# Reading the high and low slots of h by turns from two halves of the tile

## The chip, the cores and the metric

The kernel runs on one core of a Trainium2 chip. The metric is the device time of one execution in microseconds (us); before the change three runs took 3407.76, 3419.19 and 3421.75 us, the median is 3419.19. An execution taken by the hardware profiler stands beside them. Engines are named as the profile names them: PE is TensorE's matmul, PEld its weight load, DVE is VectorE, ACT is ScalarE, POOL is GpSimd, SP is SyncE, which issues the DMAs.

## The reference, cut to what matters

A model of two layers on 256 tokens and 1024 features, followed by two more blocks with large feed-forward parts. Each of the first two layers ends in a product-key expert stage. That one holds the change:

```python
def peer_ffn(x, norm_ffn, w_query, sub_keys, expert_down, expert_up):
    xn = rmsnorm(x, norm_ffn)
    ...
    q = (xi @ w_query).reshape(B, PEER_CHUNK, PEER_HEADS, 2, PEER_HALF)
    s = jnp.einsum('bthpd,hpnd->bthpn', q, sub_keys)
    s1, i1 = lax.top_k(s[..., 0, :], PEER_TOPK)
    s2, i2 = lax.top_k(s[..., 1, :], PEER_TOPK)
    ...
    g = jax.nn.softmax(top_s.astype(jnp.float32), axis=-1)
    u = jnp.take(expert_down, idx, axis=0)
    act = jax.nn.gelu(jnp.einsum('btd,bthkd->bthk', xi, u).astype(jnp.float32))
    v_sel = jnp.take(expert_up, idx, axis=0)
    return jnp.einsum('bthk,bthkd->btd', (g * act).astype(xi.dtype), v_sel)
```

There are 16384 experts, of which each token picks 16 in each of 8 heads. The kernel gathers nothing: it works through all experts densely, and the softmax weights of those not picked are zero.

## The kernel before, in words

The function `peer` runs once per layer. Its last stage is `peer_experts`, and it has two halves. In the down stretch the 16384 rows of `expert_down` are taken in 128 tiles of 128 experts; each gives a 128 x 256 tile of scores (experts by tokens), which goes through the GELU and is multiplied by the routing weights. The results stand in the tile `h`, 128 tiles of 256 tokens in fp32. In the up stretch `h` is multiplied by `expert_up`: 128 tiles again, each adding to all of the output `o_ps`, eight chunks of 128 features by 256 tokens, which fill four of the accumulator memory's eight banks, two chunks in each.

Products are made in fp32r, a one-pass form of fp32 that keeps fewer bits. To keep the accuracy each operand is cut in two, a high part (`cut_hi` on ScalarE, line 234, a copy that rounds) and a low part (`cut_lo`, line 238, the difference), and three products are added: high by high, high weights by low, low weights by high.

One tile n of the up stretch goes like this. SyncE loads 512 KB of `expert_up` into one of four slots `raw` (line 1163) once VectorE has made the low part that last read the slot. ScalarE first cuts h's tile (`cut_h`, into one of two slots `h_hi`), then the weights (into one of two slots `hi`). It waits for `out_sum`, that is for TensorE to have finished tile n - 2, whose slots it writes over. GpSimd makes `h_lo`, VectorE makes `lo` of the weights. TensorE's `accumulate` waits for the high weights and the low slot of h, makes 16 matmuls (lines 1244 and 1246: for each of eight chunks of features the high weights stand in the array, and first h_hi and then h_lo streams through), waits for the low weights and makes 8 more (line 1249). Each of the 24 matmuls has its own weight load of 128 columns and streams 256 columns of tokens.

Beside that, VectorE computes the modulation vectors of a later block from 72 more loads of 512 KB (line 1456), two products a load for the first 40 loads in layer one, one product otherwise. The first four tiles of `raw` are loaded ahead.

Where things lie: `h_hi` and `h_lo` have no tile of their own but use the normed input `K.xp`, whose content the up stretch needs no more. It is made of 2 x 8 chunks of 256 fp32r values per partition; `h_hi` is chunks 0 and 1 of the first half, `h_lo` chunks 0 and 1 of the second. A slot is 1024 consecutive bytes. The constants `LINE = 512` and `MOVED = 192` see to it that the tiles of a stage (`hi` and `lo` among them) start on multiples of 512 bytes, counted alike, and `K.xp` 192 bytes past one. A weight load reads 512 bytes per partition, from a multiple of 512.

Of the kernel before, what the change touches and what calls it, by code (L numbers as in the profile page):

```python
# [16 lines left out]
P = 128  # L17
D = 1024
DC = D // P
T = 256  # L20
# [68 lines left out]
def moving_tile(nc, stack, name, shape, dt=F32R):  # L89

    stack.enter_context(nc.sbuf_tensor(f"{name}_before", [P, MOVED // 4], F32))
    tile = padded(nc, stack, name, shape, dt, LINE)[0]
    stack.enter_context(nc.sbuf_tensor(f"{name}_after", [P, (LINE - MOVED) // 4], F32))
    return tile


class Stage:
# [135 lines left out]
def cut_hi(act, hi, v):  # L233
    return act.activation(hi, v, ACT.Copy)  # L234


def cut_lo(eng, lo, v, hi):
    return eng.tensor_tensor(lo, v, hi.bitcast(F32), ALU.subtract)  # L238
# [810 lines left out]
def peer_experts(nc, K, name, layer, dram, raw, ring):  # L1049
# [23 lines left out]
    with stage(nc, f"{name}_e") as st:  # L1073
# [9 lines left out]
        hi_up, lo_up, hi_h, lo_h, out_sum = (st.sem(x) for x in ("hi_up", "lo_up", "hi_h", "lo_h", "out_sum"))  # L1083
        hi = st.sb("hi", [P, 2, D], F32R)
        lo = st.sb("lo", [P, 2, D], F32R)
        h = st.sb("h", [P, NK, T])
# [12 lines left out]
        s = key_scores(ring)  # L1099
# [9 lines left out]
        top = choice[:, 2].rearrange("p (t h j) -> p t h j", t=TT, h=PH)  # L1109
        hots = [ring[:, i].rearrange("p (n a e) -> p n a e", n=2, a=TOKS) for i in range(RING)]  # L1110

        h_hi, h_lo = K.xp[:, 0, 0:2], K.xp[:, 1, 0:2]
        s_ps = st.ps("s", [P, D])
        c_ps = st.ps("c", [P, D])
        o_ps = st.ps("o", [P, DC, T])
# [68 lines left out]
        @block.tensor  # L1184
        def _(pe):

            def score(n, k, lo_sem, before, freed=None, freed_before=0):
                if freed is not None:
                    pe.wait_ge(freed, n - (RAWS - 1 + freed_before))
                pe.wait_ge(hi_down, n + 1)  # L1190
                out = s_banks[k]
                for c in range(DC):
                    w = hi[:, k % 2, c * P:(c + 1) * P]
                    pe.matmul(out, w, K.xp[:, 0, c], start=c == 0, stop=False)  # L1194
                    pe.matmul(out, w, K.xp[:, 1, c], start=False, stop=False)  # L1195
                pe.wait_ge(lo_sem, n + (1 - before))
                for c in range(DC):
                    mm = pe.matmul(out, lo[:, k % 2, c * P:(c + 1) * P], K.xp[:, 0, c], start=False, stop=c == DC - 1)  # L1198
                mm.then_inc(product, 1)

            for k in range(RAWS):
                score(k, k, lo_pool, 0)
            with pe.Fori(1, NS // RAWS) as i:
                for k in range(RAWS):
                    score(i * RAWS + k, k, lo_pool, 0, gelued)
            for n in range(NS, TURN_AT):
                score(n, n % RAWS, lo_vector, NS, gelued)
            pe.wait_ge(chosen, 1)
            for n in range(2):
                for t in range(TT):  # L1210
                    pe.transpose(t_ps[:, n, t * P:(t + 1) * P], pick[:, n, t], K.ident[:])
            for t in range(TT):
                mm = pe.transpose(t_ps[:, 2, t * P:(t + 1) * P],
                                  top[:, t].rearrange("p h j -> p (h j)"), K.ident[:])
            mm.then_inc(turned, 1)
            for n in range(TURN_AT, ROUTE_AT):
                score(n, n % RAWS, lo_vector, NS, gelued)

            def route(b, k, first=False):
                pe.wait_ge(hot_w, b + 1)  # L1220
                if not first:
                    pe.wait_ge(weighted, b - (G_RING - 1))
                for a in range(TOKS):
                    mm = pe.matmul(g_ps[:, k % G_RING, a * P:(a + 1) * P], hots[k][:, 0, a], hots[k][:, 1, a],
                                   start=True, stop=True)
                mm.then_inc(routed, 1)

            for k in range(RING):
                score(ROUTE_AT + k, k, lo_vector, NS, used, DIRECT)
                route(k, k, k < G_RING)  # L1230
            with pe.Fori(1, BATCHES // RING) as i:
                for k in range(RING):
                    score(i * RING + (k + ROUTE_AT), k, lo_vector, NS, used, DIRECT)
                    route(i * RING + k, k)
            for n in range(ROUTE_END, NK):
                score(n, n % RAWS, lo_vector, NS, used, DIRECT)

            def accumulate(i, k, first=False):
                n = i * RAWS + k
                pe.wait_ge(hi_up, n + 1)  # L1240
                pe.wait_ge(lo_h, n + 1)
                for c in range(DC):
                    w = hi[:, k % 2, c * P:(c + 1) * P]
                    pe.matmul(o_ps[:, c], w, h_hi[:, k % 2], start=first and c % 2 == 0, stop=False,  # L1244
                              skip_group_check=True)
                    pe.matmul(o_ps[:, c], w, h_lo[:, k % 2], start=False, stop=False, skip_group_check=True)  # L1246
                pe.wait_ge(lo_up, n + 1)
                for c in range(DC):
                    mm = pe.matmul(o_ps[:, c], lo[:, k % 2, c * P:(c + 1) * P], h_hi[:, k % 2], start=False,  # L1249
                                   stop=False, skip_group_check=True)  # L1250
                mm.then_inc(out_sum, 1)

            keep_awake(pe, K, c_ps[:, 0:P], 5)
            pe.wait_ge(weighted, BATCHES)
            pe.wait_ge(used, NK - DIRECT)
            for k in range(RAWS):
                accumulate(0, k, k == 0)
            with pe.Fori(1, BODIES) as i:
                for k in range(RAWS):
                    accumulate(i, k)  # L1260
            pe.wait_ge(mod_sum, products_before(MT))
            keep_awake(pe, K, s_ps[:, 0:P], 10)

        @block.scalar
        def _(act):
# [55 lines left out]
                cut_hi(act, hi[:, k % 2], raw[:, k]).then_inc(hi_up, 1)  # L1321

            def cut_h(n, k):
                cut_hi(act, h_hi[:, k % 2:k % 2 + 1], h[:, bass.ds(n, 1), :]).then_inc(hi_h, 1)

            act.wait_ge(product, NK - 1)
            gelu_in_place((NK - 2) % RAWS)
# [20 lines left out]
        @block.gpsimd  # L1348
        def _(pool):
            def low_down(i, k):  # L1350
                pool.wait_ge(hi_down, i * RAWS + k + 1)
                cut_lo(pool, lo[:, k % 2], raw[:, k], hi[:, k % 2]).then_inc(lo_pool, 1)

            with pool.Fori(0, NS // RAWS) as i:
                for k in range(RAWS):
                    low_down(i, k)
            pool.wait_ge(shifted, 1)
            for a in range(DIRECT, NK, 18):
                ins = pool.memset(h[:, a:a + 18], 1.0)
            ins.then_inc(ones, 1)  # L1360
            with pool.Fori(0, BODIES) as i:
                for k in range(RAWS):
                    n = i * RAWS + k
                    pool.wait_ge(hi_h, n + 1)
                    cut_lo(pool, h_lo[:, k % 2:k % 2 + 1], h[:, bass.ds(n, 1), :], h_hi[:, k % 2:k % 2 + 1])\
                        .then_inc(lo_h, 1)

        @block.vector
# [1365 lines left out]
```

## Time and profile before

| | us |
|---|---|
| median of three runs | 3419.19 |
| lowest and highest run | 3407.76, 3421.75 |
| the profiled execution | 3415.98 |
| its span, first to last instruction | 3414.2 |
| PE busy in the span | 3202.2 |
| up stretch of layer one, about | 676 to 1038 |
| up stretch of layer two, about | 1716 to 2084 |

Times in the profile's views count from the span's start. Busy times are sums of records, with overlaps counted once. Matmuls are pipelined: a record of one lasts longer than the distance to the next one's start, so distances are read from starts or from the number of records in a window, not from durations. The PEclk column is the granted clock of TensorE as a share of 2.4 GHz.

### The profile page before, as it was taken

What the parts mean: (1) busy time and instruction counts of PE and PEld (TensorE: products, weight loads), DVE (VectorE), ACT (ScalarE), POOL (GpSimd) and SP (SyncE); (2) the same over time, 40 slices, a digit from 0 to 9 for tenths busy, and PEclk for the clock granted to TensorE, in tenths of its full rate; (3) what the DMA queues carried; (4) which work ended last, traced back from release to release, by engine and by line L of the source; (5) the groups of instructions that cost most, each with busy time, mean ns of one, the idle gap of its engine ahead of it and who ended that gap; (6) DMA issues with size and microseconds to landing.
All of it is one profiled execution on the core that took longest, in us unless ns stands there. A gap on an engine that the chain in (4) does not pass through costs nothing. (4 is left out here: it accounts for less than half of the span.)

```text
span 3414.2 us, 67895 instructions
## 1 busy us (share of the span) xinstructions
PE 3202.2 (94%) x26148; PEld 3104.8 (91%) x26148; DVE 2146.2 (63%) x3339; ACT 1571.6 (46%) x2653; POOL 611.7 (18%) x478
## 2 busy tenths in 40 slices
PE   9899999999999599999999998999997789999898
PEld 8689999999998498999999998999985689999898
DVE  4659698789874749788856665333254555454654
ACT  4244576644454534466644444222144344444353
POOL 0119700033221008900022222000010010000000
PEclk9899999999999799999999999999997799999999
DMA  5145544488984135544478884222250135455353
GB/s 173 53 149 172 181 148 145 155 269 298 310 306 131 47 119 175 178 155 142 148 246 299 300 298 141 97 98 93 68 147 29 38 124 184 154 191 172 118 191 129
DMA packets 178906, 560.78 MB, mean 164 GB/s; under 512 B 22480, under 2 KB 31440, under 8 KB 178144
## 3 DMA queue, kind: packets, MB, share of 16 engines
q1 hardware_dynamic: 178784, 559.21, 49.8%
q8 instruction: 69, 1.13, 0.1%
q14 instruction: 53, 0.43, 0.0%
HBM read 558.10 MB, written 1.05 MB: 164 GB/s over the span
## 5 line engine op out<-in xcount | busy, mean ns | idle before, releaser
L234 ACT ACTIVATE peer_e_hi<-peer_raw 128x1024 fp32r<-128x1024 f32 x512 | 539.0, 1053 | 357.1 <-PE peer_e_o L1198 172.1
L238 DVE TENSOR_TENSOR peer_e_lo<-peer_raw,peer_e_hi 128x1024 fp32r<-128x1024 f32 x416 | 516.9, 1245 | 289.4 <-ACT peer_e_hi L234 289.0
L238 DVE TENSOR_TENSOR ffn_lo<-ffn_raw,ffn_hi 128x1024 fp32r<-128x1024 f32 x260 | 318.4, 1226 | 494.1 <-ACT ffn_hi L234 494.1
L234 ACT ACTIVATE ffn_hi<-ffn_raw 128x1024 fp32r<-128x1024 f32 x264 | 279.8, 1061 | 540.6 <-PE ffn_acc L2028 341.6
L1244 PE MATMUL peer_e_o<-x_normed,peer_e_hi 128*128 128x256 f32 x2048 | 490.4, 280 | 10.1 <-ACT peer_e_hi L234 8.7
L1246 PE MATMUL peer_e_o<-x_normed,peer_e_hi 128*128 128x256 f32 x2048 | 489.8, 280 | 0.0
L1244 PEld LDWEIGHTS peer_e_o<-x_normed,peer_e_hi 128*128 128x128 f32 x2048 | 388.7, 190 | 10.8 <-ACT peer_e_hi L234 9.1
L238 POOL TENSOR_TENSOR x_normed<-peer_e_h,x_normed 128x256 fp32r<-128x256 f32 x256 | 209.0, 816 | 1049.5 <-ACT x_normed L234 1049.5
L1246 PEld LDWEIGHTS peer_e_o<-x_normed,peer_e_hi 128*128 128x128 f32 x2048 | 388.8, 190 | 0.0
L2019 PE MATMUL ffn_acc<-x_normed,ffn_hi 128*128 128x256 f32 x1408 | 352.1, 281 | 10.5 <-DVE x_normed L332 6.8
L2020 PE MATMUL ffn_acc<-x_normed,ffn_hi 128*128 128x256 f32 x1408 | 349.0, 279 | 0.0
L238 POOL TENSOR_TENSOR peer_e_lo<-peer_raw,peer_e_hi 128x1024 fp32r<-128x1024 f32 x96 | 269.2, 2814 | 126.8 <-ACT peer_e_hi L234 125.5
L1249 PE MATMUL peer_e_o<-x_normed,peer_e_lo 128*128 128x256 f32 x2048 | 281.5, 280 | 2.2 <-DVE peer_e_lo L238 1.6
L2019 PEld LDWEIGHTS ffn_acc<-x_normed,ffn_hi 128*128 128x128 f32 x1408 | 268.6, 191 | 15.5 <-POOL x_normed L238 6.7
L234 ACT ACTIVATE x_normed<-peer_e_h 128x256 fp32r (+1 forms) x256 | 107.0, 418 | 361.5 <-PE peer_e_o L1249 361.5
L2020 PEld LDWEIGHTS ffn_acc<-x_normed,ffn_hi 128*128 128x128 f32 x1408 | 268.8, 191 | 0.0
L1249 PEld LDWEIGHTS peer_e_o<-x_normed,peer_e_lo 128*128 128x128 f32 x2048 | 256.8, 189 | 4.3 <-DVE peer_e_lo L238 4.0
L1194 PE MATMUL peer_e_s<-x_normed,peer_e_hi 128*128 128x256 f32 x1024 | 249.1, 285 | 6.9 <-ACT peer_e_hi L234 6.9
L1194 PE MATMUL peer_e_o<-x_normed,peer_e_hi 128*128 128x256 f32 x1024 | 246.9, 283 | 0.0
L1195 PE MATMUL peer_e_s<-x_normed,peer_e_hi 128*128 128x256 f32 x1024 | 243.1, 279 | 0.0
L1195 PE MATMUL peer_e_o<-x_normed,peer_e_hi 128*128 128x256 f32 x1024 | 241.4, 278 | 0.0
L2028 PE MATMUL ffn_acc<-x_normed,ffn_lo 128*128 128x256 f32 x1408 | 225.6, 278 | 0.0
(620 smaller groups left out, 7529.4 us busy)
## 6 DMA issues: line engine op xcount, KB each, us to landing
peer_raw<-in_l_down SPq DMA_DIRECT2D x256, 512.0 KB, 3.5
peer_raw<-in_l_up SPq DMA_DIRECT2D x256, 512.0 KB, 4.8
ffn_raw<-in_ffn_wi SPq DMA_DIRECT2D x176, 512.0 KB, 3.4
peer_ring<-in_w_mod SPq DMA_DIRECT2D x144, 512.0 KB, 5.1
ffn_raw<-in_ffn_wo SPq DMA_DIRECT2D x88, 512.0 KB, 3.5
l_in_raw<-in_l_w_in SPq DMA_DIRECT2D x39, 512.0 KB, 4.3
peer_q_raw<-in_l_peer_w_query SPq DMA_DIRECT2D x32, 512.0 KB, 4.7
wg_in_raw<-in_w_in SPq DMA_DIRECT2D x26, 512.0 KB, 3.7
```

Source lines behind the costliest of these rows:

```text
L234: return act.activation(hi, v, ACT.Copy)
L238: return eng.tensor_tensor(lo, v, hi.bitcast(F32), ALU.subtract)
L1194: pe.matmul(out, w, K.xp[:, 0, c], start=c == 0, stop=False)
L1195: pe.matmul(out, w, K.xp[:, 1, c], start=False, stop=False)
L1244: pe.matmul(o_ps[:, c], w, h_hi[:, k % 2], start=first and c % 2 == 0, stop=False, skip_group_check=True)
L1246: pe.matmul(o_ps[:, c], w, h_lo[:, k % 2], start=False, stop=False, skip_group_check=True)
L1249: mm = pe.matmul(o_ps[:, c], lo[:, k % 2, c * P:(c + 1) * P], h_hi[:, k % 2], start=False, stop=False, skip_group_check=True)
L2019: pe.matmul(at, w, x.pair[:, 0, c], start=c == 0 and s == 0, stop=False, skip_group_check=True)
L2020: pe.matmul(at, w, x.pair[:, 1, c], start=False, stop=False, skip_group_check=True)
L2028: mm = pe.matmul(out[:, s * T:(s + 1) * T], w, x.pair[:, 0, c], start=False, stop=c == DC - 1, skip_group_check=True)
```

## The change

The slots of h move within `K.xp`. All four (high and low, two slots each) are now in two halves by tokens: tokens 0 to 127 of each slot lie in the first 2048 bytes, tokens 128 to 255 lie 4160 bytes further on, which is eight times 512 and 64 more. A slot's half is 512 bytes. The matmuls of the up stretch read the two halves by turns, 16 columns (64 bytes) from the one and 16 from the other, and write the accumulator in the same order, so that every token's result ends up where it was. In layer one the pieces are taken from first to last, in layer two from last to first, the two halves in the same order within each pair. ScalarE's and GpSimd's cuts of h read and write the same values as two runs of 128.

```diff
+PIECE = 16
+
+
+def alternating(a, step):
+
+    return a.rearrange("p two (l e) -> p l two e", e=PIECE)[:, ::step]
...
-        h_hi, h_lo = K.xp[:, 0, 0:2], K.xp[:, 1, 0:2]
+        ahead, between, step = ((0, T * 4 + PIECE, 1), (0, T * 4 + PIECE, -1))[layer]
+        h_pair = K.xp[:].rearrange("p u c t -> p (u c t)")[:, ahead:ahead + 2 * between]\
+            .rearrange("p (two s) -> p two s", two=2)[:, :, 0:4 * P].rearrange("p two (u k t) -> p u k two t", u=2, k=2)
+        h_hi, h_lo = h_pair[:, 0], h_pair[:, 1]
+        h_halves = h[:].rearrange("p n (two t) -> p n two t", two=2)
+        o_halves = lambda c: alternating(o_ps[:, c].rearrange("p (two t) -> p two t", two=2), step)
...
-                    pe.matmul(o_ps[:, c], w, h_hi[:, k % 2], start=first and c % 2 == 0, stop=False,
+                    pe.matmul(o_halves(c), w, alternating(h_hi[:, k % 2], step), start=first and c % 2 == 0, stop=False,
                               skip_group_check=True)
-                    pe.matmul(o_ps[:, c], w, h_lo[:, k % 2], start=False, stop=False, skip_group_check=True)
+                    pe.matmul(o_halves(c), w, alternating(h_lo[:, k % 2], step), start=False, stop=False,
+                              skip_group_check=True)
                 pe.wait_ge(lo_up, n + 1)
                 for c in range(DC):
-                    mm = pe.matmul(o_ps[:, c], lo[:, k % 2, c * P:(c + 1) * P], h_hi[:, k % 2], start=False,
-                                   stop=False, skip_group_check=True)
+                    mm = pe.matmul(o_halves(c), lo[:, k % 2, c * P:(c + 1) * P], alternating(h_hi[:, k % 2], step),
+                                   start=False, stop=False, skip_group_check=True)
...
-                cut_hi(act, h_hi[:, k % 2:k % 2 + 1], h[:, bass.ds(n, 1), :]).then_inc(hi_h, 1)
+                cut_hi(act, h_hi[:, k % 2:k % 2 + 1], h_halves[:, bass.ds(n, 1)]).then_inc(hi_h, 1)
...
-                    cut_lo(pool, h_lo[:, k % 2:k % 2 + 1], h[:, bass.ds(n, 1), :], h_hi[:, k % 2:k % 2 + 1])\
+                    cut_lo(pool, h_lo[:, k % 2:k % 2 + 1], h_halves[:, bass.ds(n, 1)], h_hi[:, k % 2:k % 2 + 1])\
```

## Rows read from the trace of the kernel before

**Rows 1.** The page, part 1: busy us (share) x instructions of each engine.

```profile
PE 3202.2 (94%) x26148; PEld 3104.8 (91%) x26148; DVE 2146.2 (63%) x3339; ACT 1571.6 (46%) x2653; POOL 611.7 (18%) x478
```

**Rows 2.** Waits, 676 to 1038, then 1716 to 2084: us in total, times, longest.

```profile
PE peer_e_o L1244 <- ACT peer_e_hi L234: 4.9, 1, 4.9
PEld peer_e_o L1249 <- DVE peer_e_lo L238: 4.0, 9, 1.0
PE peer_e_o L1249 <- DVE peer_e_lo L238: 1.6, 2, 0.8
...
POOL x_normed L238 <- ACT x_normed L234: 269.0, 127, 4.9
ACT x_normed L234 <- PE peer_e_o L1249: 184.2, 124, 3.2
...
PE peer_e_o L1244 <- ACT peer_e_hi L234: 3.9, 1, 3.9
```

**Rows 3.** Windows, PE alone: us, PE busy (records), clock, DMA share, GB/s.

```profile
677.00:687.00 10.00, 10.00 (x88) 1.00 0.01 4
853.00:887.00 34.00, 34.00 (x291) 1.00 0.90 296
890.00:1038.00 148.00, 148.00 (x1308) 1.00 0.84 287
1740.00:2080.00 340.00, 340.00 (x2889) 1.00 0.86 288
2120.00:2340.00 220.00, 220.00 (x1944) 1.00 0.29 96
2565.00:2575.00 10.00, 10.00 (x91) 1.00 0.36 131
1732.00:1736.00 4.00, 4.00 (x21) 0.50 0.79 278
```

**Rows 4.** Timeline around 850 us: start, us, engine, line, operation, [idle before].

```profile
849.78 2.90 DVE L238 TENSOR_TENSOR peer_e_lo<-peer_raw,peer_e_hi 128x1024 fp32r<-128x1024 f32 x2
849.86 1.73 POOL L238 TENSOR_TENSOR x_normed<-peer_e_h,x_normed 128x256 fp32r<-128x256 f32 x1 [1.79 <-ACT x_normed L234]
...
850.67 0.28 PE L1246 MATMUL peer_e_o<-x_normed,peer_e_hi 128*128 128x256 f32 x1
...
851.05 1.21 PE L1249 MATMUL peer_e_o<-x_normed,peer_e_lo 128*128 128x256 f32 x8
852.10 0.28 PE L1244 MATMUL peer_e_o<-x_normed,peer_e_hi 128*128 128x256 f32 x1
```

**Rows 5.** Timeline of a run of 64-column matmuls, the first, second and seventh.

```profile
1062.02 0.28 PE L243 MATMUL l_in_acc<-l_in_hi,x_normed 128*128 128x64 f32 x1
1062.13 0.28 PE L244 MATMUL l_in_acc<-l_in_lo,x_normed 128*128 128x64 f32 x1
...
1062.69 0.28 PE L243 MATMUL l_in_acc<-l_in_hi,x_normed 128*128 128x64 f32 x1
```

**Rows 6.** Timeline (all, then from the second) and durations of line 854's matmuls.

```profile
104.18 1.67 PE L854 MATMUL hgrn_a<-hgrn_pair,hgrn_onehot 128*8 128x448 f32 x4
...
104.56 1.29 PE L854 MATMUL hgrn_a<-hgrn_pair,hgrn_onehot 128*8 128x448 f32 x3
...
106.42 1.88 PE L854 MATMUL hgrn_a<-hgrn_pair,hgrn_onehot 128*8 128x512 f32 x4
...
L854 PE MATMUL hgrn_a<-hgrn_pair,hgrn_onehot x32: 276/461/596, 93.4 to 107.7; 128*8 128x64 f32 x4, 128*8 128x128 f32 x4, 128*8 128x192 f32 x4, 128*8 128x256 f32 x4
```

**Rows 7.** Layer two: line 238 on POOL (min/median/max ns), the cut of h.

```profile
L238 POOL TENSOR_TENSOR x_normed<-peer_e_h,x_normed x127: 738/745/1379, 1716.0 to 2079.5; 128x256 fp32r<-128x256 f32 x127
...
L234 ACT ACTIVATE x_normed<-peer_e_h 128x256 fp32r x124 | 51.9, 418 | 179.8 <-PE peer_e_o L1249 179.8
```

## The prediction, made before the changed kernel ran

> **What bounds the kernel now.** I read the page first, then the groups by line, then windows cut inside the changed stretches, then single instructions. TensorE is busy for 94% of the span [rows 1], and no other engine or queue comes near. The two up stretches (676 to 1038 us and 1716 to 2084 us) hold 3072 of these matmuls each: 128 tiles of 24. Who waits for whom there [rows 2]: in layer one TensorE waits 4.9 us for ScalarE once (behind a DMA), then only 1.6 us in two waits for VectorE's low halves; in layer two it waits 3.9 us once and never again. ScalarE and GpSimd, which make the high and low slots of h, wait 184.2 and 269.0 us in all in layer two, so they are early. What the up stretches cost is therefore the number of matmuls times the distance between two starts.
>
> That distance comes from windows. A matmul's record is 0.28 us long and records overlap, so a window of W us holds (W + 0.28) / distance records. Layer one, 890 to 1038: 148.28 / 1308 = 113.4 ns. Layer one, 853 to 887: 34.28 / 291 = 117.8 ns; 677 to 687 about 117 ns. Layer two, 1740 to 2080: 340.28 / 2889 = 117.8 ns [rows 3]. The same instruction with the same shape thus has two levels, 4.4 ns apart, and the clock is 1.00 in all of them. Transfers don't choose the level: the feed-forward stage runs 220.28 / 1944 = 113.3 ns at 96 GB/s and layer one 113.4 ns at 287 GB/s [rows 3]. What comes ahead of a switch is a pause: at 850.67 TensorE waits for the low half that VectorE is late with, the next start is 851.05, and the window that follows is the one at 117.8 ns [rows 3, 4]. Once it streams without a pause, the level stays, as over layer two's 340 us.
>
> Neither level is the array's own rate. At granted clock 0.50 (1.2 GHz, after that one wait) 4.42 / 21 = 210 ns fit 256 columns at 1.2 GHz (213.3) with nothing on top [rows 3]; half of it, 106.7, is what the array would need at 2.4 GHz. The upper levels have 6.7 and 11.1 ns more: here the array waits for its operands. Two more rows split this. With only 16 stationary columns, 10.28 / 91 = 113 ns: the 6.7 ns belong to the moving stream itself. With only 64 moving columns the starts lie 0.11 to 0.12 us apart, 0.67 us over six, 112 ns: that is what loading 128 stationary columns costs [rows 3, 5]. Weights and moving columns are read side by side; the second level looks like the two meeting in some part of the memory, at a phase that the last pause set.
>
> **The change, step by step.** Nothing is added to or taken from any queue: 6144 matmuls, 256 cuts on ScalarE, 256 on GpSimd, the same waits and DMAs. Changed are addresses and order.
>
> 1. The matmuls. Before, one reads 1024 consecutive bytes while the weights behind it read 512. Now it takes 64 bytes of one half and 64 of the other, whose place within 512 is one piece on, so in 16 pieces its place within 512 moves by 512, as the weights' does. Forward, the two run in step and needn't meet; backward they run against each other and pass quickly. If it works, the second level goes. Layer two: 3072 less the two score that ran at 0.50 or around it, 3030, times 117.8 - 113.3 = 4.45 ns: 13.5 us. Layer one: 34 us of it, 289 matmuls, and some 70 at its start, 360 x 4.45 = 1.6 us. Together 15.1 us. That is one end of what it gives. The other: that part of the moving stream's own 6.7 ns goes too, down to what the weights need, 111.7 to 112 ns. That is 1.65 ns on 6060 matmuls, 10 us more, 25.1 in all. The trace has no single-pass matmul that reads in pieces; between these two I take the middle, 20 us, since the weights' row stands next to it.
>
> 2. The cost of the jumps. The nearest rows are the pair matmuls of the first mixer (two-pass fp32, 64 runs of 7 columns with a gap after each, read and written that way): 1.67 - 1.29 = 0.38 us for 448 columns, against (1.88 - 0.59) / 3 = 0.43 us for 512 columns without gaps, 0.59 us being the longest record of the line [rows 6]. Per column that is 0.84 and 0.84 ns: 64 gaps cost nothing. Those columns come at half the rate, though. So the lower bound is 0, the upper one array cycle (0.42 ns, from 106.7 / 256) for each of 16 pieces, 6.7 ns a matmul, 41 us on 6144. I take 0 by the row.
>
> 3. ScalarE's cut of h takes 418 ns, GpSimd's 745 ns in the middle and 1379 at most in layer two [rows 7]. The new form is two runs of 128 in place of one of 256. By the row of gaps above I take nothing; if each run cost as one instruction, 0.84 us. It is hidden behind the matmuls of the tile between: in the tile shown GpSimd has 1.73 us at 849.86, done at 851.59, and the next tile's matmuls start at 852.10, half a microsecond to spare in the worst kind of tile, a whole one otherwise [rows 4]. Were the cover gone, 0.3 us in some 25 such tiles: 8 us.
>
> 4. What a faster TensorE runs into. Layer two loads at 288 GB/s at 117.8 ns; at 112 to 113.3 it asks for 300 to 303. Layer one's transfers sustain this with no wait after the first tiles [rows 2, 3]. Layer one's waits for VectorE (9 on the weight side, 4.0 us) hang on VectorE's two products a tile, stay, and may grow by 0.1 us each: 1 us. They redraw the level under the old order; layer two, with one product a tile, has none.
>
> Sum: -20 us with bounds -25 and -15 by step 1, +0 to +41 by step 2, +0 to +9 by steps 3 and 4. The profiled execution took 3415.98 us (span 3414.2), 3.2 below the median of 3419.19. 3416.0 - 20 = 3396, plus 3.2 gives 3399.
>
> The Trainium skill has a rule against step 1: "SBUF — State Buffer", Who interferes with whom, says that TensorE and ScalarE wait for nobody at the memory's ports, and gives its weights and its moving operand ports of their own. By it the order of reading can't matter and the sum is 0. The trace has two levels for one instruction, 113.4 and 117.8 ns, which that rule doesn't explain; it leaves the first rival its chance.
>
> **The rivals.**
>
> No measurable change (chance 0.28): the phase is drawn anew at a pause and the new order has two levels as well. Layer one then may stand at the upper one: 2712 matmuls x 4.45 = +12.1 against -13.5 in layer two, about 3418. For it: the level flips with a pause alone, and the three runs of before lie 14 us apart (3407.76 to 3421.75), as one stretch's level would make. Against it: in step, two streams keep whatever distance the pause left them, 192 or 256 bytes by the layout if they start together.
>
> Slower (chance 0.19): the pieces interrupt a stream that is already short of data. Place: the moving read or the accumulator's write, all 6144 matmuls; price: one array cycle a piece, +41 us with nothing won, 3460. It decides from 20 us / 6144 / 16 = 0.2 ns a piece, half a cycle. For it: this stream, unlike the pair matmuls, runs above what its supply gives (6.7 ns over). Against it: 64 gaps at no cost [rows 6]. "PSUM — Partial Sum Buffer", Specifications (TRN2), supports this rival: it says that any access pattern that isn't contiguous slows matmuls a good deal. The pair matmuls, written in runs of 7, don't show that.
>
> Down to the array's rate (chance 0.05): weights and moving data both lose their surplus, 106.7 ns: layer two 3030 x 11.1 = 33.6, layer one 360 x 11.1 + 2670 x 6.7 = 21.9, together -55, 3364. Against it: the weights' 112 ns.
>
> **How the numbers follow.** The forecast (3394 to 3404, 3399 in the middle) has 0.48. What a measurement here can tell from no change is about 0.5%, 17.1 us, so below 3402 is faster: about four fifths of the forecast (0.38), the deep case (0.05) and a little of the second level's luck (0.03), 0.46. Within: the rest of the forecast (0.10), most of the first rival (0.23), 0.33. Slower: the second rival and 0.02 of the first, 0.21. For 8 in 10 the range starts 15 us under the forecast and reaches up to the slow case at half its price (+20): 3384 to 3438. Of the forecast alone it would be 3390 to 3408.
>
> **What would show it.** Windows of 148 and 340 us as above: distances of 112 to 113.3 ns in both layers, and no stretch of 117.8 in layer two. 113.3 in both says the second level went alone (3404). 117.8 left in either says phase still rules. Distances of 120 or more say that pieces cost, equal in both layers if it is the jump, unlike if it is the direction. The cut on ScalarE should stay at 418 ns and TensorE should have no new wait for GpSimd in layer two. Layer two's transfers should pass 300 GB/s. The prediction is wrong if the distances stay and the time moves, or if a wait for h appears.

## The result, and the profile after

Seven runs of the changed kernel have a median of 3440.31 us (3431.99 to 3456.08), seven of the kernel before, the three known ahead among them, 3410.51 us (3402.88 to 3425.21). The ratio is 1.0089 with a 95% interval of 1.0062 to 1.0116: slower by 0.9%, 30 us, where a gain of 20 us had been forecast. The profiled execution has a span of 3450.2 us against 3414.2.

First the windows of the changed kernel, TensorE alone; columns and reading as in [rows 3]: us, busy (records), granted clock, DMA share, GB/s, and the distance of two starts is (window + 0.28) / records.

```profile
677.00:687.00 10.00, 10.00 (x85) 1.00 0.01 3
853.00:887.00 34.00, 34.00 (x286) 1.00 0.86 291
890.00:1038.00 148.00, 148.00 (x1236) 1.00 0.86 291
1760.00:2100.00 340.00, 340.00 (x2836) 1.00 0.86 285
2140.00:2360.00 220.00, 220.00 (x1871) 1.00 0.28 91
```

In the up stretches that is 148.28 / 1236 = 120.0 ns and 340.28 / 2836 = 120.0 ns, in layer one as in layer two, where [rows 3] have 113.4 and 117.8 ns in layer one and 117.8 ns in layer two. There is one level now, whatever the pause before (from the first row 10.28 / 85 = 120.9 ns, from the second 119.9). The last row is the first feed-forward stage, which the change doesn't touch: 220.28 / 1871 = 117.7 ns, 113.3 before.

Then the matmuls of the first of the three lines (duration in ns min/median/max, first and last start), layer one and two of the kernel before, then of the changed one.

```profile
L1244 PE MATMUL peer_e_o<-x_normed,peer_e_hi x1024: 276/276/497, 676.0 to 1037.4; 128*128 128x256 f32 x171
...
L1244 PE MATMUL peer_e_o<-x_normed,peer_e_hi x1024: 281/281/582, 1715.6 to 2083.1; 128*128 128x256 f32 x171
```

```profile
L1257 PE MATMUL peer_e_o<-x_normed,peer_e_hi x1024: 282/283/572, 675.5 to 1049.4; 128*128 128x256 f32 x171
...
L1257 PE MATMUL peer_e_o<-x_normed,peer_e_hi x1024: 278/285/582, 1731.1 to 2104.2; 128*128 128x256 f32 x171
```

Layer one's up stretch went from 361.4 to 373.9 us, layer two's from 367.5 to 373.1: +12.5 and +5.6, 18 of the 36 us between the spans. Another 3.5 us lie between the two stretches and 14.9 us behind the second. Two causes can be named for these, with estimates that are rough and together come out somewhat above them. One is the feed-forward stage at the upper level: 220 us / 113.3 ns x 4.4 ns = 8.5 us in its window alone. The other is the clock: mean granted clocks of 0.966 and 0.963 make 232 and 255 us at 1.2 GHz, if the clock has only its two levels, and half of the difference, 12 us (give or take 3 for the rounding), is lost time. The stage's level also changes between kernels that don't touch it (below, at the kernel before once more), and the mean clock of 17 runs of the kernel before lay between 0.963 and 0.968 by itself. So I don't put either down to the change.

Of the changed kernel's up stretch of layer two: its waits (us in total, times, longest), GpSimd's cut of h (ns min/median/max), and ScalarE's (busy us, mean ns):

```profile
ACT x_normed L242 <- PE peer_e_o L1263: 189.9, 124, 3.0
...
POOL x_normed L246 <- ACT x_normed L242: 274.9, 127, 5.0
...
PE peer_e_o L1257 <- ACT peer_e_hi L242: 3.8, 1, 3.8
...
PE peer_e_o L1257 <- POOL x_normed L246: 0.7, 1, 0.7
```

```profile
L246 POOL TENSOR_TENSOR x_normed<-peer_e_h,x_normed x127: 734/742/1369, 1731.5 to 2100.5; 128x256 fp32r<-128x256 f32 x127
```

```profile
L242 ACT ACTIVATE x_normed<-peer_e_h 128x256 fp32r x124 | 51.8, 418 | 185.4 <-PE peer_e_o L1263 185.4
```

Against [rows 2, 7] hardly anything moved: the cut on ScalarE takes 418 ns as before, GpSimd's 742 for 745. ScalarE waits a little longer for TensorE, and GpSimd for ScalarE. The one wait for GpSimd is 0.7 us long and stands at the start of the stretch. It isn't new: [rows 2] begin at 1716 us, just behind it, and with the window opened at 1714 us the kernel before has the same line.

```profile
PE peer_e_o L1244 <- POOL x_normed L238: 0.7, 1, 0.7
```

In layer one, these are all the waits of TensorE's matmuls in the changed kernel, from 675 to 1050 us:

```profile
PE peer_e_o L1257 <- ACT peer_e_hi L242: 4.6, 1, 4.6
...
PE peer_e_o L1257 <- POOL x_normed L246: 0.7, 1, 0.7
```

The waits for VectorE's low halves, 1.6 us on the matmul side and 4.0 us on the weight side in [rows 2], are gone: at 120.0 ns TensorE is slow enough for VectorE to keep up. So the matmuls' distance accounts for the longer stretches, and in layer one it even hides some of its cost in pauses that no longer occur.

### The profile page after: what moved, and what is told of

Same layout as the page of the kernel before. It is cut to its first block and busy times, and to the rows that moved or that the text cites. A ratio compares the mean times of both kernels' runs of the same rounds, so it can differ in the third digit from the quotient of the medians.

```text
span 3450.2 us, 67895 instructions
## 1 busy us (share of the span) xinstructions
PE 3241.4 (94%) x26148; PEld 3142.9 (91%) x26148; DVE 2141.0 (62%) x3339; ACT 1571.6 (46%) x2653; POOL 600.6 (17%) x478
## 5 line engine op out<-in xcount | busy, mean ns | idle before, releaser
L1257 PE MATMUL peer_e_o<-x_normed,peer_e_hi 128*128 128x256 f32 x2048 | 505.7, 284 | 9.8 <-ACT peer_e_hi L242 8.4
L1259 PE MATMUL peer_e_o<-x_normed,peer_e_hi 128*128 128x256 f32 x2048 | 505.0, 284 | 0.0
L246 POOL TENSOR_TENSOR x_normed<-peer_e_h,x_normed 128x256 fp32r<-128x256 f32 x256 | 197.6, 772 | 1078.6 <-ACT x_normed L242 1078.6
L1263 PEld LDWEIGHTS peer_e_o<-x_normed,peer_e_lo 128*128 128x128 f32 x2048 | 263.8, 190 | 0.0
L1207 PE MATMUL peer_e_o<-x_normed,peer_e_hi 128*128 128x256 f32 x1024 | 247.0, 283 | 0.0
L1208 PE MATMUL peer_e_o<-x_normed,peer_e_hi 128*128 128x256 f32 x1024 | 241.5, 278 | 0.0
```

Of the source, the lines that this page charges most:

```text
L1257: pe.matmul(o_halves(c), w, alternating(h_hi[:, k % 2], step), start=first and c % 2 == 0, stop=False, skip_group_check=True)
L1259: pe.matmul(o_halves(c), w, alternating(h_lo[:, k % 2], step), start=False, stop=False, skip_group_check=True)
L1263: mm = pe.matmul(o_halves(c), lo[:, k % 2, c * P:(c + 1) * P], alternating(h_hi[:, k % 2], step), start=False, stop=False, skip_group_chec ...
```

## The experiments

In most of them the two layers are set differently, so that one kernel tells two things. Distances are read in windows from 900 to 1030 us (layer one) and 1760 to 2060 us (layer two), both in every trace inside the stretches. Each is one profiled execution, except the whole change with pieces of 256 bytes, which was timed over twelve. "Distance" is how far the slot starts behind the place where the weights start, and "parts" are the 64 bytes at 0, 64, 128 and 192 modulo 256.

**Write or read (e1).**

Layer one has its slots in their old place, reads them straight and writes in pieces. Layer two has its slots in halves, reads in pieces and writes straight (cut to two lines):

```diff
...
+            else (lambda c: o_ps[:, c])
+        read = (lambda a: a.rearrange("p two t -> p (two t)")) if layer == 0 else (lambda a: alternating(a, step))
```

> Layer one writes the accumulator in 16 pieces and reads its slot straight through, from the old place; layer two reads in 16 pieces and writes straight (tokens land out of order in both, so the sums are not the reference's). After the change both layers stand at 120.0 ns a matmul, 2880 a tile of 24, against 113.3 or 117.8 before. Theory read: the jumps of the moving read cost one array cycle (0.417 ns) each: layer one goes back to 113.3 or 117.8 (2720 or 2827 a tile), layer two stays at 120. Rival write: it is the accumulator's write in pieces: layer one stands at 120, layer two at 113.3 or 117.8. If both cost, both stand at 117 or more and neither level of before is seen.

```profile
900.00:1030.00 130.00, 130.00 (x1150) 1.00 0.88 299
1760.00:2060.00 300.00, 300.00 (x2502) 1.00 0.88 294
```

130.28 / 1150 = 113.3 ns with pieces written, 300.28 / 2502 = 120.0 ns with pieces read. The whole cost is in the read. Writing the accumulator in 16 runs of 64 bytes costs nothing. "PSUM — Partial Sum Buffer", Specifications (TRN2), in the Trainium skill, which the prediction cited for the slow rival, says that any access pattern that isn't contiguous slows matmuls a good deal. At this size of run the measurement doesn't bear it out.

**The size of the pieces (e2, e6).** `PIECES = (32, 64)`, then `(8, 4)`, halves 64 bytes apart, forward.

> Halves 64 bytes apart as in the change, read forward in both layers, in 8 pieces of 32 columns in layer one and 4 pieces of 64 in layer two. Theory jumps: 113.3 + 0.417 a piece: 116.7 ns in layer one (2800 a tile), 115.0 in layer two (2760). Rival lockstep: what costs is that the stream runs at the weights' pace and meets them again and again; pieces of 32 and 64 break the pace and both layers return to the two levels, 113.3 or 117.8. Rival flat: any broken pattern costs the same, 120 in both.

> The change, forward in both layers, with 32 pieces of 8 columns (32 bytes) in layer one and 64 pieces of 4 (16 bytes) in layer two. Theory ceiling: 120.0 is what a stream without any run-on gets, since 16 and 32 columns a piece gave the same: 120.0 in both layers. Rival count of jumps: the cost is per jump, with something that hid it between 32 and 16 columns: 120 plus 0.417 for each further piece, 126.7 in layer one and 140 in layer two.

The first kernel:

```profile
900.00:1030.00 130.00, 130.00 (x1086) 1.00 0.88 294
1760.00:2060.00 300.00, 300.00 (x2560) 1.00 0.89 299
```

The second:

```profile
900.00:1030.00 130.00, 130.00 (x1066) 1.00 0.86 287
1760.00:2060.00 300.00, 300.00 (x2461) 1.00 0.86 288
```

For 4, 8, 16, 32 and 64 pieces that is 117.3, 120.0, 120.0, 122.2 and 122.0 ns. So there is no price per jump: 8 and 16 pieces cost the same, and 64 pieces no more than 32. The jump theory (116.7, 115.0, 126.7, 140) missed all four, the ceiling of 120 missed both of its own (122.2 and 122.0), and the rival of a broken pace missed layer one's 120.

**The distance of the halves, and the directions (e3, e4).** First `between = (T * 4, T * 4 + 4 * PIECE)`, then `step = (-1, 1)`.

> Pieces of 16, forward in both layers, only the distance of the halves differs: 4096 bytes in layer one (same place within 512), 4352 in layer two (half of 512 further on). Theory jumps: 120.0 ns in both, whatever the distance. Rival place: the memory has parts by address, and the 64 bytes decide: then the two layers differ from each other and from 120 by more than 1 ns.

> The change with its directions exchanged, backward in layer one and forward in layer two. Theory jumps: 120.0 ns in both; the direction only changes how single distances scatter (in the change forward shows 119 to 121 in turns, backward 115 to 126, both 120.0 on average). Rival direction: one of the layers leaves 120 by more than 1 ns.

Both kernels stand at 120.0 ns in both layers (1086 and 2502 records; 1086 and 2503). Direction doesn't matter, and for pieces of 16 columns neither does it whether the halves are 0, 64 or 256 bytes apart modulo 512. The jump theory had this right, but the kernels with other pieces refute its price per jump; what is left of it is a flat 120.0 ns for these turns.

**One jump, and jumps within a slot (e5).**

Layer one has its old slots and takes pieces of 16 columns from the last to the first; layer two has its halves 4160 bytes apart and takes one after the other.

```diff
+        if layer == 0:
...
+            order = lambda a: a.rearrange("p two t -> p (two t)").rearrange("p (l e) -> p l e", e=PIECE)[:, ::-1]
+        else:
+            order = lambda a: a
```

> Layer one: slots in their old place, 1024 bytes each, read and written in pieces of 16 columns from the last to the first: 16 jumps, all within the slot. Layer two: halves far apart as in the change, but read one after the other, one jump. The read in pieces has cost 120.0 ns for 16 and for 8 pieces and 117.4 for 4, so it is not 0.417 ns a jump. Theory broken read (any order that isn't straight through): 120 in layer one; in layer two between 113.3 and 117.4. Rival two places: what costs is to go between two places 4160 bytes apart: layer one stands at 113.3 or 117.8, layer two up to 120.

```profile
900.00:1030.00 130.00, 130.00 (x1106) 1.00 0.87 294
1760.00:2060.00 300.00, 300.00 (x2502) 1.00 0.87 293
```

Fifteen jumps within a slot: 117.8 ns. One jump between halves: 120.0 ns. The count of jumps explains nothing, and the theory of a broken read fell in both layers. The rival of two places far apart held in both; the halves 4096 bytes apart (e14, below) refute it. What the second read has besides and the first hasn't is bytes that begin 64 further on. Whether 117.8 ns is the reversed order's own level or the upper of the old two, one execution doesn't tell.

**A straight read from another place (e7, e8, e13, e15).** The kernel before, with this changed alone:

```diff
-        h_hi, h_lo = K.xp[:, 0, 0:2], K.xp[:, 1, 0:2]
+        ahead = (16, 32)[layer]
+        h_hi, h_lo = (K.xp[:, u].rearrange("p c t -> p (c t)")[:, ahead:ahead + 2 * T]
+                      .rearrange("p (k t) -> p k t", k=2) for u in range(2))
```

and in three further kernels `ahead` of (48, 80), (64, 96) and (8, 60).

> The kernel before, read straight through, with all slots of h 64 bytes further on in layer one and 128 bytes in layer two. Theory of my prediction (weights and moving columns meet in parts of the memory by address): the upper level or its share of tiles changes, at least one layer shows a level other than 113.3 and 117.8 (say 115 or 120). Rival: place doesn't matter, only the phase after a pause: the same two levels, 113.3 and 117.8, in whatever share.

> The kernel before, read straight through, slots of h 192 bytes further on in layer one and 320 in layer two. So far: 0 bytes 113.3 or 117.8, 64 bytes 120.0, 128 bytes 117.8. Theory meeting: the distance decides, and other distances have other levels, from 113.3 to 120; one may hold 113.3 in all tiles. Rival: 113.3 or 117.8 wherever the distance isn't 64.

> The kernel before, read straight through, slots of h 256 bytes further on in layer one (distance to the weights' line 448) and 384 in layer two (distance 64). Theory: levels repeat every 256 bytes, as 128 and 384 gave the same 118.7: layer one stands at 113.3 or 117.8 as at 192, layer two at 117.8 as at 320. Rival: the period is 512, and 128 and 384 agree by chance: at least one of the two shows another level.

> The kernel before, read straight through, slots of h 32 bytes further on in layer one (distance 224) and 240 in layer two (distance 432, which is 176 if levels repeat every 256). Theory: parts of 64 bytes: 224 lies in the same part as 192 at its start and crosses into the next sooner, a level between 113.3 and 120; 176 lies 16 bytes before, also between 113.3 and 118.7. Rival: only the 64-byte part of the start counts: layer one 113.3 or 117.8 like 192, layer two 118.7 like 128.

The first of them; its layer one matters most:

```profile
900.00:1030.00 130.00, 130.00 (x1085) 1.00 0.86 290
1760.00:2060.00 300.00, 300.00 (x2549) 1.00 0.89 300
```

And the third:

```profile
900.00:1030.00 130.00, 130.00 (x1150) 1.00 0.83 287
1760.00:2060.00 300.00, 300.00 (x2549) 1.00 0.88 298
```

In the third, layer one also has a stretch at 110.28 / 936 = 117.8 ns:

```profile
770.00:880.00 110.00, 110.00 (x936) 1.00 0.86 298
```

In layer one of the first kernel not a byte is out of order, yet its distance of two starts is 130.28 / 1085 = 120.1 ns: moving the slot by 64 bytes costs as much as the change does. The full map, by the distance of the slot from a 512-byte line, where the weights start:

| bytes modulo 512 | modulo 256 | ns a matmul |
|---|---|---|
| 192 (before), 448 | 192 | 113.3 or 117.8, both within a stretch |
| 224 | 224 | 118.3 (x1101) |
| 256, 0 | 0 | 120.1, 120.0 (x1085, x2503) |
| 320, 64 | 64 | 117.8, 117.8 (x2549 each) |
| 384 | 128 | 118.8 (x1097) |
| 432 | 176 | 119.3 (x2518) |

Three pairs of places 256 bytes apart agree, so the levels repeat every 256 bytes, and bytes between the multiples of 64 count too. The place before has the lowest level of the six places modulo 256 that were tried. Two things stay unsure. For 64, both executions stood at 117.8 ns throughout, which is also the upper level of 192; whether it has a lower one isn't known. And the other places have one execution each, or two. Of the expectations, "levels repeat" held; "the same two levels wherever the distance isn't 64" and "only the 64-byte part of the start counts" fell. The forecast of a level between two others held for 224 and missed for 176 (119.3 ns, above both of its neighbours' values).

**Place in memory, or distance to the weights (e10).** Tiles `hi` and `lo` 64 bytes further on in both layers, slots 64 further on in layer one only. The stage's other tiles move too; of them the matmuls of the up stretch read none.

> The kernel before with the tiles of the weights (hi, lo) 64 bytes further on in both expert stages, and the slots of h 64 bytes further on in layer one, in their old place in layer two, all read straight through. Slots 64 bytes further on with the weights in place stood at 120.0. Theory meeting: only the distance of the two streams counts: layer one returns to 113.3 or 117.8, layer two leaves both levels (it has the distance 128, not tried yet). Rival address: layer one stands at 120, layer two at 113.3 or 117.8.

```profile
900.00:1030.00 130.00, 130.00 (x1149) 1.00 0.91 307
1760.00:2060.00 300.00, 300.00 (x2530) 1.00 0.86 292
```

Layer one's slots stand where 120.1 was measured, but the weights moved along, and it is back at 113.4 ns. Layer two's slots are at their old place, and 300.28 / 2530 = 118.7 ns, the level of distance 128. So the distance of two streams decides, not an address: the moving columns and the weights read beside them are in each other's way. Both layers came out as the theory of meeting had said. "SBUF — State Buffer", Who interferes with whom, in the Trainium skill says that TensorE waits for nobody there and that its two reads have ports independent of each other. These two rows contradict it for TensorE's own two reads.

**Fewer weights (e9).** `w = hi[:, k % 2, c * P:c * P + 16]`: 16 stationary columns, the change's read in layer one, the straight read 64 bytes on in layer two.

> All matmuls of the up stretches with 16 stationary columns in place of 128 (only 16 of each 128 output features are computed). Layer one reads as in the change, forward; layer two reads straight through from slots 64 bytes further on. Both kinds of read stood at 120.0 ns with 128 stationary columns. Theory meeting: what costs beyond 113.3 is that the weights are read beside the moving columns: both layers drop to 113.3. Rival stream alone: the order and the start address slow the moving read by themselves: both stay at 120.

```profile
900.00:1030.00 130.00, 130.00 (x1066) 1.00 0.86 288
1760.00:2060.00 300.00, 300.00 (x2574) 1.00 0.87 297
```

Its first group of weight loads in layer one, 700 to 1030 us (count, busy us, mean ns):

```profile
L1263 PEld LDWEIGHTS peer_e_o<-x_normed,peer_e_hi 128*16 128x16 f32 x903 | 86.4, 96 | 23.8
```

A weight load is 96 ns instead of some 190, and the matmuls are at 130.28 / 1066 = 122.2 and 300.28 / 2574 = 116.7 ns, where 128 columns gave 120.0 and 120.1. Narrower weights helped one order and hurt the other. Neither theory had that. So the number of weight bytes read doesn't by itself set the cost. The kernel also writes only 16 of the accumulator's partitions, so what exactly made the difference isn't separated here.

**An order by turns that stays clear (e12, e16, e17).** If the two in step kept a fixed distance, some distance should be free. First all slots of the change 128 and 256 bytes on, then halves 128 and 192 bytes apart, each at two distances. Each of the three kernels replaces one line of the change (the place of the slots, the distance of the halves and the direction, for layer one and layer two):

```diff
-        ahead, between, step = ((0, T * 4 + PIECE, 1), (0, T * 4 + PIECE, -1))[layer]
+        ahead, between, step = ((32, T * 4 + PIECE, 1), (64, T * 4 + PIECE, 1))[layer]
...
+        ahead, between, step = ((0, T * 4 + 2 * PIECE, 1), (PIECE, T * 4 + 2 * PIECE, 1))[layer]
...
+        ahead, between, step = ((0, T * 4 + 3 * PIECE, 1), (2 * PIECE, T * 4 + 3 * PIECE, 1))[layer]
```

> The change, forward in both layers, with all its slots 128 bytes further on in layer one and 256 in layer two. Theory meeting, in the form of my prediction (in step the two streams don't meet, at some distance): at least one of the layers drops to 113.3 or below, to 112. Rival: a broken read gets 120 at any distance, as it did with the halves 0, 64 and 256 bytes apart: 120.0 in both.

> The change, forward in both layers, with halves 128 bytes apart (modulo 512) in place of 64: the parts of 64 bytes modulo 256 come in the order 3 1 0 2 1 3 2 0, in layer two one further on: 0 2 1 3 2 0 3 1. Weights go through 0 0 1 1 2 2 3 3 in the same time. Theory repetition: the change costs 120 since it reads each part twice in a row; here none comes twice, so 113.3 or less in both. Theory meeting in step: with the right distance the two never share a part: one of the layers drops to 112 to 113.3, the other, which always shares one, stands at 120 or above. Rival: turns of 16 columns cost 120 in any arrangement.

> As e16 with halves 192 bytes apart: parts 3 2 0 3 1 0 2 1 in layer one, everything two parts further on (1 0 2 1 3 2 0 3) in layer two. Again no part twice in a row. Theory repetition: 113.3 or less in both. Theory meeting in step: one layer at 112 to 113.3, the other at 120 or above. Rival: 120 in both, as for the halves 0, 64 and 256 apart.

In this order:

```profile
900.00:1030.00 130.00, 130.00 (x1066) 1.00 0.85 288
1760.00:2060.00 300.00, 300.00 (x2499) 1.00 0.86 290
...
900.00:1030.00 130.00, 130.00 (x1056) 1.00 0.86 285
1760.00:2060.00 300.00, 300.00 (x2503) 1.00 0.86 289
...
900.00:1030.00 130.00, 130.00 (x1086) 1.00 0.87 291
1760.00:2060.00 300.00, 300.00 (x2502) 1.00 0.87 294
```

Layer one and two: 122.2 and 120.2 ns, 123.4 and 120.0 ns, 120.0 and 120.0 ns. Nothing stands at or below 113.3 ns; one is at the highest level of all, with no part read twice in a row. If weights and columns start together, all three layer ones never share a part, by the sequences in the expectations (the first of them, two parts on from the change's, has 1 2 2 3 3 0 0 1 against 0 0 1 1 2 2 3 3). So meeting in step, as I had pictured it, is refuted, and so is the repetition of a part as the cause. The rival's "120 in any arrangement" is near, but missed 122.2 and 123.4.

**Halves and turns in the parts' old order (e14).** Halves exactly 4096 bytes apart, a multiple of 256; layer one reads one after the other, layer two in 4 pieces of 64 columns.

> Halves of the slots exactly 4096 bytes apart, both at the good distance of 192. Layer one reads one half after the other (one jump), layer two takes 4 pieces of 64 columns in turns. Theory place: only where each stretch of bytes stands against the weights counts. Layer one reads the same places in the same order as a straight slot, so 113.3 or 117.8; in layer two the second piece starts where the first did, half of the bytes come out of step with the straight order, and it leaves these levels. Rival jump: a jump costs by itself: layer one too stands above 117.8, at 120.0 as it did with halves 64 bytes apart.

```profile
900.00:1030.00 130.00, 130.00 (x1150) 1.00 0.89 303
1760.00:2060.00 300.00, 300.00 (x2650) 1.00 0.91 310
```

Both layers stand at 113.3 ns. I had expected layer two off the levels; but a piece of 64 columns is 256 bytes, so the second piece goes through the same four parts again, and modulo 256 the order is that of a straight read. One jump and three jumps over 4096 bytes are thus free, which refutes the rival of the jump, and with it the rival of e5, two places far apart. Together with the shifted straight read and the shifted weights this leaves the order of addresses modulo 256 and its distance to the weights as what decides. Not separated from it is a price of short runs by themselves: turns of 16 columns can't have the parts' straight order, and the only other read in runs of 64 bytes, backward within the slot, stood at 117.8 ns.

**The whole change with that one property restored, timed (e18).**

```diff
-PIECE = 16
+PIECE = 64
...
-        ahead, between, step = ((0, T * 4 + PIECE, 1), (0, T * 4 + PIECE, -1))[layer]
+        ahead, between, step = ((0, T * 4, 1), (0, T * 4, -1))[layer]
```

> The change with its halves, turns and directions (forward in layer one, backward in layer two), but pieces of 64 columns (256 bytes) and halves exactly 4096 bytes apart, so that the parts modulo 256 come in the order of a straight read. Theory sequence of parts: both layers at 113.3 or 117.8 as before the change, up stretches of 354 to 370 us each, and the time that of before: ratio 0.997 to 1.003. Rival: turns or the backward direction keep a cost of their own that the look at four forward pieces missed: layer two above 118 ns, ratio 1.005 or more.

```profile
900.00:1030.00 130.00, 130.00 (x1150) 1.00 0.87 297
1760.00:2060.00 300.00, 300.00 (x2649) 1.00 0.91 310
```

113.3 and 113.4 ns, median 3416.48 us (3407.62 to 3431.73) against 3412.15 of before, ratio 1.0017 with an interval of 0.9994 to 1.0040: the loss of 0.9% is gone, with halves, turns and the backward direction all kept. It takes both edits: pieces of 16 with halves 4096 bytes apart stood at 120.0 ns, pieces of 64 with halves 4160 apart at 117.3 ns.

**The kernel before, once more (b2_before).**

> The kernel before once more, nothing changed, to see whether a stretch keeps its level from execution to execution. Theory drawn levels: each stretch of layer two, and each feed-forward stage, stands at 113.3 or 117.8 as the pause before it left it, so layer two's up stretch may be 354 us long this time in place of 368.5. Rival fixed levels: the same tiles at the same levels as in the first profile, layer two all at 117.8.

```profile
L1244 PE MATMUL peer_e_o<-x_normed,peer_e_hi x1024: 276/281/582, 669.8 to 1038.6; 128*128 128x256 f32 x171
...
L1244 PE MATMUL peer_e_o<-x_normed,peer_e_hi x1024: 276/276/415, 1727.3 to 2080.7; 128*128 128x256 f32 x171
```

```profile
1760.00:2060.00 300.00, 300.00 (x2650) 1.00 0.90 311
2150.00:2330.00 180.00, 180.00 (x1531) 1.00 0.28 92
```

Layer two's stretch is 353.4 us this time, not 367.5, at 113.3 ns; layer one's is 368.8, not 361.4; the feed-forward stage is at 180.28 / 1531 = 117.8 ns, not 113.3. Levels are drawn anew in each execution. The feed-forward stage stood at 113.3 ns in most kernels of the study and at 117.8 ns in the changed one, this one and four others (e3, e10, e14, e17), without any bearing on what was edited. Nor is it the chip: e5, e6 and e7 ran on the same one as b2_before, and their stage is at 113.3 ns. That is where the feed-forward part of the 36 us belongs.

The traces show two more things about these levels. First, they change at pauses. In layer one of the kernel before, from 700 us on, the starts of TensorE's matmuls have thirteen pauses; at four of them, 763.0, 771.8, 850.7 and 887.9 us, the level changes, and nowhere between. Second, the draw isn't even. In all eleven up stretches that read at distance 192 in the straight order, the first four tiles stand at 117.8 ns, and behind the pause that follows ten go on at 113.3 ns and one, layer two of the first profile, at 117.8 ns. The profile that the prediction was read from had the rare case.

## Why the prediction was wrong

**What bounds the kernel:** right. TensorE hardly waits; the time is the number of matmuls times a distance, and in the changed kernel too.

**Two levels, set by a pause, kept while the stream runs on:** right, and the same within one program from run to run. But then the 117.8 ns of layer two were one draw, and the 13.5 us counted as removable there aren't there in every execution: over the two profiles of before, the stretches take 728.9 and 722.2 us together, and 714.6 us in the kernel with pieces of 256 bytes (361.5 and 353.1), with the change 747.0. The cost is thus 18 to 32 us, by the draw. Since layer two's stretch took 353.1 and 353.4 us in the two later profiles at 113.3 ns and 373.1 us with the change, about 20 us there and 12.5 in layer one make an estimate of 32 us for the common case, near the 30 us between the medians. The first rival, no measurable change, was right that the levels are drawn and wrong that the new order has two of them.

**Step 1, the failed one:** "Forward, the two run in step and needn't meet; backward they run against each other and pass quickly." The premise that the two reads are in each other's way by their distance is right. That they are free of each other when they run in step is wrong, and so is the -15 to -25 us that hung on it: ten settings of turns of 16 columns were measured (halves 0, 64, 128, 192 and 256 bytes apart, both directions, several distances), and all stand at 120.0 to 123.4 ns, where the sum had 112 to 113.3. The picture had the wrong period: 256 bytes, not 512. Weights and turns both pass it twice a matmul, and with the change's layout (parts 3 0 0 1 1 2 2 3 against 0 0 1 1 2 2 3 3) every other piece would have met the weights even in my own picture. That isn't the whole error: e12, e16 and e17 show that moving the turns to a clear distance doesn't help either. And the 6.7 ns that the prediction gave to the moving stream alone, from a row with 16 stationary columns, aren't a fixed share: e9 has 122.2 and 116.7 ns with 16.

**Step 2, the jumps:** the value of 0 was right for the jumps themselves, though it came from a matmul at half the rate [rows 6]; e14 and e18 show it at full rate for up to three jumps. The slow rival had the right place (the moving read) and by chance the right price: 113.3 + 6.7 = 120.0. Its mechanism, an array cycle a piece, is refuted by e2, e5 and e6. It gave 3460 against the measured 3440.31: it added its 41 us to a profile whose layer two was already at the upper level, and to a median of three runs, 3419.19, that seven runs put at 3410.51.

**Steps 3 and 4:** the cuts and their cover behaved as stated. Layer one's waits for VectorE did not stay; with the slower matmuls they went. TensorE got no faster, so the transfers weren't tested by the change. In b2_before, layer two's loads ran at 311 GB/s between 1760 and 2060 us, where the first profile had 300, and TensorE waited no more for it than before (3.9 us once), as step 4 had reckoned.

**The range** reached up to the slow case at half its price; the time lies 2 us outside. The weight of 0.48 on the forecast had one picture behind it and no row of a matmul that reads in pieces at full rate.

What stays open: why a straight read has 113.3 ns where the array needs 106.7, what sets 117.8 after a pause, and by which rule the two reads delay each other. The map and e9 don't agree with shared parts alone. Whether turns of 64 bytes have a price of their own beside their order stays open too.

## What to carry to other kernels

Where fp32r matmuls run back to back, look at the distance of their starts, not at their durations or the engine's busy share: several levels, 4 to 6% apart from lowest to highest, can hide under "94% busy". The place of the moving columns relative to the weights, modulo 256 bytes, moved it here from 113.3 to 120.1 ns with not a byte reordered; try the places once for a straight read before touching the order. Before comparing two kernels by one profile each, look whether stages that were not edited changed level.

## What the runs showed that was not expected

- A straight single-pass fp32r read of 256 columns takes 113.3 to 120.1 ns by its distance to the weights modulo 256, six distances tried; the same instruction at a granted clock of 0.50 stands at 210 ns [rows 3], which fits 256 columns at 1.2 GHz (213.3 ns) with nothing on top.
- Shrinking the weights from 128 to 16 columns made the read by turns slower, 120.0 to 122.2 ns, and a straight one faster, 120.1 to 116.7.
- Writing the accumulator in 16 runs of 64 bytes cost nothing (113.3 ns).
- A read in 64 pieces of 16 bytes costs only 122.0 ns, 7.7% over the lower level of a straight one.
- A straight stream has two levels, 113.3 and 117.8 ns, that change only at a pause of TensorE, and an execution that got the rare one made 13.5 of the forecast's 20 us look removable.
